# Seven block products instead of eight in all six feed-forwards, and a new order of the vector work

## The reference

```python
def swiglu(h, w1, w3, w2):
    return (jax.nn.silu(h @ w1) * (h @ w3)) @ w2
def half_ffn(x, g, w1, w3, w2):
    return x + FFN_RES * swiglu(rmsnorm(x, g), w1, w3, w2)     # four times in the first block
...
    for l in range(DEPTH):                                      # second block
        mod = (c_act @ w_ada[l] + b_ada[l])[:, None, :]
        sh1, sc1, g1, sh2, sc2, g2 = jnp.split(mod, N_MOD, axis=-1)
...
        x = x + g2 * swiglu_2(h, w_gate_up[l], w_down[l])
```

## Time and profile before

| | us |
|---|---|
| median of 3 runs (lowest, highest) | 3132.42 (3131.48, 3132.74) |
| the profiled execution | 3134.22 |
| its span, first to last instruction | 3132.4 |
| busy TensorE, VectorE, ScalarE | 3120.2, 2040.7, 1274.8 |

### The profile page before, as it was taken

One profiled execution on the slowest core, in us unless ns is written; L12 is line 12 of the kernel. 1 busy time (PEld: TensorE's weight loads), 2 busy tenths in 40 slices (PEclk: granted clock), 3 DMA queues, 4 the chain that ended last, 5 costly groups with the idle time before them and its releaser, 6 DMA issues.

```text
span 3132.4 us, 39304 instructions
## 1 busy us (share of the span) xinstructions
PE 3120.2 (100%) x15840; PEld 2629.8 (84%) x15840; DVE 2040.7 (65%) x3069; ACT 1274.8 (41%) x1908; POOL 156.5 (5%) x170
## 2 busy tenths in 40 slices
PE   9999999999999999999999999999999999999999
PEld 7888878888888888888888888887898988789898
DVE  5457567445755456647644575888893868889574
ACT  5322264322234222264332223556452545745342
POOL 2000000000000000000000000113000002400000
PEclk9999999999999999999999999999999999999999
DMA  5345422334542335422233454221223233022322
GB/s 151 94 134 180 136 85 88 101 94 135 189 141 82 104 125 168 155 94 82 81 100 102 135 181 146 69 81 39 83 95 118 86 103 97 15 94 94 109 92 84
DMA packets 334348, 340.00 MB, mean 109 GB/s; under 512 B 12503, under 2 KB 329209, under 8 KB 334169
## 3 DMA queue, kind: packets, MB, share of 16 engines
q1 hardware_dynamic: 332144, 333.80, 33.4%
q0 software_dynamic: 1792, 3.62, 0.4%
q10 hardware_dynamic: 232, 0.06, 0.0%
HBM read 335.36 MB, written 2.10 MB: 108 GB/s over the span
## 4 chain that ended last, share of the span: by engine, by line
PE 92%; DVE 4%; ACT 3%; DMA 0%; issue 0%; SPq 0%; DVEq 0%
PE ps L138 90%; PE ps L141 2%; ACT ar L95 1%; DVE wl L100 1%; DVE ar L108 1%; DVE ar L100 1%; ACT wh L95 0%; DVE hl L108 0%; DMA raw<-in_ffn_w 0%; DVE T L108 0%; ACT L95 0%; ACT sp L95 0%; ACT T L95 0%; DVE ar L123 0%; DVE ar L111 0%
## 5 line engine op out<-in xcount | busy, mean ns | idle before, releaser
L100 DVE TENSOR_TENSOR wl<-raw,wh 128x1024 fp32r<-128x1024 f32 (+3 forms) x709 | 728.4, 1030 | 421.0 <-ACT wh L95 418.9
L138 PE MATMUL ps<-hh,wl 128*128 128x512 f32 (+1 forms) x2632 | 991.7, 377 | 2.0 <-DVE wl L100 1.1
L138 PE MATMUL ps<-hh,wh 128*128 128x512 f32 (+1 forms) x2632 | 984.7, 374 | 0.0
L138 PE MATMUL ps<-hl,wh 128*128 128x512 f32 (+1 forms) x2632 | 984.3, 374 | 0.0
L95 ACT ACTIVATE wh<-raw 128x1024 fp32r<-128x1024 f32 (+3 forms) x709 | 628.4, 896 | 536.2 <-PE ps L138 458.7
L138 PE MATMUL ps<-ul,wh 128*128 128x512 f32 (+1 forms) x1664 | 585.4, 356 | 0.0
L138 PEld LDWEIGHTS ps<-hh,wl 128*128 128x128 f32 x2632 | 496.0, 188 | 95.9 <-issue 8.2
L138 PEld LDWEIGHTS ps<-hh,wh 128*128 128x128 f32 x2632 | 496.0, 188 | 88.9
L138 PEld LDWEIGHTS ps<-hl,wh 128*128 128x128 f32 x2632 | 496.3, 189 | 85.6 <-issue 0.2
L138 PE MATMUL ps<-uh,wl 128*128 128x512 f32 (+1 forms) x1568 | 557.3, 355 | 0.8 <-ACT sq L95 0.8
L138 PE MATMUL ps<-uh,wh 128*128 128x512 f32 (+1 forms) x1568 | 555.9, 354 | 0.0
(11 more groups left out here) (258 smaller groups left out, 2898.6 us busy)
## 6 DMA issues: line engine op xcount, KB each, us to landing
raw<-in_ffn_w SPq DMA_DIRECT2D x119, 1024.0 KB, 5.3
raw<-in_w_ada SPq DMA_DIRECT2D x48, 1024.0 KB, 5.2
raw<-in_w_gate_up SPq DMA_DIRECT2D x44, 1024.0 KB, 5.1
raw<-in_m_w_in SPq DMA_DIRECT2D x26, 1024.0 KB, 5.4
raw<-in_w_down SPq DMA_DIRECT2D x16, 1024.0 KB, 5.2
raw<-in_ffn_w SPq DMA_DIRECT2D x16, 768.0 KB, 4.9
raw<-in_w_in SPq DMA_DIRECT2D x12, 1024.0 KB, 5.4
raw<-in_m_w_out SPq DMA_DIRECT2D x8, 1024.0 KB, 5.2
```

What stands on the lines that cost most here:

```text
L100: return self.issue(lambda e: e.tensor_tensor(out, a, b, op))
L138: return self.issue(lambda e: e.matmul(out, l, r, start=start, stop=stop, skip_group_check=True))
```

## The change

WOVEN now holds the same 16 chunks for all six stages (32 before, 96 after), so the four ffn stages take the woven form with its two output parts. The description says 17 chunks; the set in the code has 16. ADA_AFTER becomes a table: 10 conditioning chunks in each ffn stage and 8 in ffn2 of layer 0, all in the first output part; the waits for them ask for number 23 in layer 0. The splits get due times of their own: blocks 6 and 5 one and two steps later, the mixes as entries of the same sorted list lo_order, and ScalarE goes by hi_order. The gates of ffn and ffn2 become a step of their own (`gated` on VectorE), done one step after the join, and the low parts two steps later (settle).

```diff
+WOVEN = {s: {("w3", 2), *((w, j) for j in range(3, 11) for w in ("w1", "w3"))} - {("w3", 10)} for s in FFNS}
 PARTS = (1, 4, 6, 5)
-ADA_AFTER = ({("post", "w3", 2 * j + 1) for j in range(7, 11)} | {("out", (k0, kt), 2 * m + 1) for m in range(3) for k0, kt in ((0, 8), (8, 8), (16, 6)) if m < 2 or k0 < 16},
-             {("post", "w3", 15), ("post", "w3", 19), *(("out", k, t) for k in ((0, 8), (8, 6)) for t in (1, 3, 5, 7)), ("out", (14, 8), 1), ("out", (14, 8), 3)})
+ADA_AFTER = {s: {("out", k, t): 1 + (s[0] == "ffn" and (k, t) in (((0, 8), 3), ((8, 6), 5))) for k in ((0, 8), (8, 6)) for t in (1, 3, 5, 7)}
+             for s in FFNS[:5]}
+ADA_AFTER[FFNS[5]] = {}
 SHARE = {1: (0, 0), 5: (0, 0), 3: (0, 0), 2: (1, 0), 4: (1, 1), 6: (1, 1), 7: (0, 1)}
 MOVING = {5: 0, 6: 1, 7: 2, 4: 3}
 BETWEEN = [("xb", 4), ("xb", 5), ("xb", 6), ("xb", 7), ("z", 2), ("z", 3)]
...
+        def plan_ffn(key, w1, w3, w2):
             at = {}
             for what, w, i, p in rounds(key):
                 j = i if what in ("part", "joined") else i // 2
...
             elif st[0] == "mix0":
                 W = I['m0_w_in'][0]
...
+        due = {g: before[g] + 1 for g in before}
+        for g, (s, w, j, p) in part_of.items():
+            if p in (6, 5):
+                due[g] = min(due[g] + (1 if p == 6 else 2), g - 2)
+        hi_order = sorted(due, key=lambda g: (due[g], g))
+        lo_order, last = [], 0
+        for o in order:
+            if o[0] == "ada":
+                lo_order.append((max(due[last], 2), last, 1, o))
+            else:
+                last = o[1]
+                lo_order.append((due[last], last, 0, o))
+        for g, (s, w, j, p) in part_of.items():
+            at_part = {c: due[G_of[(s, w, j, "part", c)]] for c in (1, 3, 4, 5)}
+            if p == 1:
+                lo_order.append((due[g], g, 1, ("mix", 7, part_of[g], shape[g][0])))
+            elif p == 4:
+                lo_order.append((due[g] + 1, -3, 0, ("mix", 6, part_of[g], shape[g][0])))
+                lo_order.append((due[g] + 1, -1, 0, ("mix", 5, part_of[g], shape[g][0])))
+            elif p == 3:
+                late = at_part[3] - 2 <= at_part[5]
+                lo_order.append((max(at_part[3] - 2, at_part[5]), g if late else -2, 1, ("mix", 3, part_of[g], shape[g][0])))
+        lo_order.sort(key=lambda c: c[:3])
...
-            mms = [o for o in order if o[0] == "mm"]
...
-                while at[0] < len(mms) and before[at[0]] < g:
-                    i = at[0]
+                while at[0] < len(hi_order) and due[hi_order[at[0]]] <= g:
+                    i = hi_order[at[0]]
...
-                for _ in range(3 if s == STAGES[0] else 4):
+                for _ in range(1 if s[0] == "ffn" else 4):
...
+                        dve.wait_ge(*left_of(("ada", 47 if s[1] else 23)))
                         if s[0] == "ffn2":
...
-
-                if p == 1:
-                    mix(7, 1, 7, SUB)
-                elif p == 4:
+            def mixed_weights(dst, chunk, n):
+
+                s, w, j, _ = chunk
+                a, b, op = {7: (1, 7, SUB), 6: (4, 7, SUB), 5: (6, 1, ADD), 3: (2, 6, SUB)}[dst]
+                if dst == 6:
                     dve.wait_ge(worked, (s, w, j, 7, "weights"))
                     dve.wait_ge(lo_split, G_of[(s, w, j, "part", 4)])
-                    mix(6, 4, 7, SUB)
-                    dve.own()
-                    mix(5, 6, 1, ADD)
-                elif p == 7:
+                elif dst == 5:
+                    dve.wait_ge(worked, (s, w, j, 6, "weights"))
+                    dve.wait_ge(lo_split, G_of[(s, w, j, "part", 1)])
+                elif dst == 3:
+                    dve.wait_ge(worked, (s, w, j, 6, "weights"))
                     dve.wait_ge(lo_split, G_of[(s, w, j, "part", 5)])
-                    mix(3, 2, 6, SUB)
+                dve.tt(quarter_of(n, dst), quarter_of(n, a), quarter_of(n, b), op).then_inc(worked, (s, w, j, dst, "weights"))
 
             def split_ahead(g):
 
...
-                    o = order[at[0]]
-                    if (before[o[1]] >= g) if o[0] == "mm" else (g < 2):
-                        return
+                while at[0] < len(lo_order) and lo_order[at[0]][0] <= g:
+                    o = lo_order[at[0]][3]
                     at[0] += 1
                     if o[0] == "mm":
                         hi, lo, src = split_views(o[1])
                         dve.wait_ge(hi_split, o[1])
                         dve.tt(lo, src, hi.bitcast(F32), SUB).then_inc(lo_split, o[1])
-                        if o[1] in part_of:
-                            mixed_weights(*part_of[o[1]], o[2])
+                    elif o[0] == "mix":
+                        mixed_weights(*o[1:])
                     else:
                         _, i, n = o
                         src = raw_view(n)
...
+
+            def gated(s, w, t):
+
+                to = (T1 if w == "w1" else T3)[t % 2][:, :]
+                done = (worked, (s, "odd", w, t // 2)) if t % 2 else left_of((s, "Y", w, t // 2))
+                dve.wait_ge(*done)
+                if w == "w1":
                     dve.tt(to, to, R[:, :], MUL).then_inc(worked, (s, "gate", t))
-                if w == "w3":
-                    dve.own()
+                else:
                     silu_done(s, t)
-                    dve.tt(to, to, T1[a][:, :], MUL).then_inc(worked, (s, "gv", t))
+                    dve.tt(to, to, T1[t % 2][:, :], MUL).then_inc(worked, (s, "gv", t))
 
             def differences(s):
-                if s != STAGES[0]:
+                if s[0] == "ffn2":
                     yield 1
                 for q in range(4):
...
+                    token = dve.beside(differences(s))
+                    if s[0] == "ffn":
+                        next(token)
+                        next(token)
                 chain, later = None, []
+
+                def settle():
+                    for c in list(later):
+                        c[0] -= 1
+                        if c[0] == 0:
+                            later.remove(c)
+                            if c[1] == "low":
+                                low_gated(s, c[2])
+                            else:
+                                gated(s, *c[1:])
+                                if c[1] == "w3":
+                                    later.append([2, "low", c[2]])
+
                 for what, w, i, p in rounds(s):
                     if what == "run":
                         product(s, w, i)
...
                     elif what == "joined":
                         joined(s, w, i, p)
-                        if w == "w3":
-                            later.append(2 * i + p)
+                        if w == "w3" or s[0] == "ffn":
+                            later.append([1, w, 2 * i + p])
                     elif what == "out":
...
-                        while later:
-                            low_gated(s, later.pop(0))
+                        settle()
+                        while later and p & 2:
+                            settle()
                         if p & 2:
                             added(s, nxt, i, p)
...
-                pool.wait_ge(used, G_of[(BEFORE[s], "w2", 14 if WOVEN[BEFORE[s]] else 0, 7)])
+                pool.wait_ge(used, G_of[(BEFORE[s], "w2", *((14, 0) if WOVEN[BEFORE[s]] else (0, 7)))])
```

More of the change, by code:

```diff
@@ L371, in plan_ffn @@
                     n_mm[0] += 1
-                if with_ada and (what, w, i) in ADA_AFTER[bool(WOVEN[key])]:
-                    plan_ada(1)
+                plan_ada(ADA_AFTER[key].get((what, w, i), 0))
         for st in STAGES:
             if st[0] == "ffn":
-                plan_ffn(st, I['ffn_w1'][st[1], st[2]], I['ffn_w3'][st[1], st[2]], I['ffn_w2'][st[1], st[2]], True)
+                plan_ffn(st, I['ffn_w1'][st[1], st[2]], I['ffn_w3'][st[1], st[2]], I['ffn_w2'][st[1], st[2]])
             elif st[0] == "mix0":
```

17 lines of the change are left out of this document (4 added, 13 removed).

## The result

| | before | after |
|---|---|---|
| median, us (lowest, highest) | 3132.38 (3131.48, 3132.74) | 3227.08 (3226.18, 3231.43) |
| the profiled execution, its span | 3134.22, 3132.4 | 3231.43, 3229.6 |
| busy TensorE, VectorE, ScalarE | 3120.2, 2040.7, 1274.8 | 3101.2, 2473.5, 1470.9 |

The change makes the kernel slower: ratio 1.0306, interval 1.0288 to 1.0323. The forecast was 3175, with a range of 3147 to 3200; it is 52 us short. The page of the changed kernel, for the earlier trace rows: span; busy time and count of the engines; the chain by engine; the group of the low splits, with VectorE's idle time before them and what ended it.

The account below looks back on a forecast made before the run. The prediction took VectorE's handing over with ScalarE to bound the woven rounds. From the profiled execution: 3134.2 - 52 + 71 + 11 + 2.5 + 8.6 + 2 = 3177.3; with the median 1.8 lower, 3175 us, range 3147 to 3200.

Parts of the forecast that it names:

- TensorE's part: 64 chunks go from plain to woven form, 10.90 to 10.08 us each: 52 us less if TensorE is fed.
- VectorE's round: Woven ffn chunks take 11.85 us, 1.77 over TensorE's 10.08, through waits for ScalarE: 71 us lost in four stages.
- A: TensorE stays the bound; waits for ScalarE fall into VectorE's free time in woven rounds: 3093 us, chance 0.07.
- B: One of the round's two waits is hidden because ScalarE takes its silu earlier: 3123 to 3147 us, chance 0.09.
- D: VectorE instructions cost their full duration in woven rounds, 0.687 for 0.604 us: 3244 us, chance 0.02.
- E: Matmuls of 256 columns cost 0.130 us, so seven products save nothing: 3145 us with rounds hidden, chance 0.01.
- the low part of tile 12: First output part: TensorE waits for it at the fifth tile of (8,6), 1.6 us in five stages, 8.6 in all.
- the part's account of 79.2 us: First output part: VectorE's conditioning, splits, additions and chunk ends sum to 78.5 of 79.2 us, so full.
- Rival C: First output part overflows, VectorE waiting for ScalarE and TensorE: 5 us more in each of four stages, 3195 us, chance 0.12.
- The first chunks and the constants: The first stage's constants, some 15 instructions at 0.16 us, stand in the woven rounds: 2.5 us.
- ffn2: Its woven chunks under the new order take 10.64 us, 0.56 over before's 10.08: 11 us lost in 20 steps.
- The gathering matmul: First output part: the reduce waiting for it makes a split 1 us late in ffn (0,1) and (1,1): 2 us.

Follow-up runs that it names:

- number 1: Changed kernel with ScalarE's silu (or high part of u) one step later, behind the next high splits, and VectorE's low part one step later: 3130.02 us.
- 4: Changed kernel with only the odd tile's silu (or high part of u) behind the next high splits on ScalarE, low part alike: 3173.99 us.
- number 2: Changed kernel with VectorE doing waiting gates and low parts ahead of splits and conditioning at the second output of each part: 3193.21 us.
- number 3: Changed kernel with both edits: ScalarE's silu behind the next high splits, and VectorE's gates and low parts ahead of the conditioning: 3097.55 us.
- Number 5: Changed kernel with the old WOVEN and old conditioning table, so the new order alone, the four ffn stages in plain chunks: 3150.66 us.

## Why the prediction was wrong, step by step

**TensorE's part** held: -52, and matmuls of 256 columns 0.120 us apart.

**VectorE's round** held in mechanism and size: 11.85 us forecast, 11.83 measured; waits of 1.31 and 0.70 forecast, 1.30 and 0.70 measured, both ended by ScalarE's wh; TensorE's gap before each block 6 was forecast at 1.8 and is 1.53 of idle time, 1.69 over the usual step. Numbers 1 and 4 show the chain by taking it away. Rivals A, B, D and E are out: A and B by the waits in each round, D by the starts 0.60 apart (1123.46, 1124.06), E by the 0.120.

**The term that failed is the low part of tile 12**: 1.6 us a stage forecast, 5.16 measured in the four ffn stages and 4.88 in ffn2 of layer 0, and behind it 1.5 to 2.9 from the clock (in ffn (1,0) 2.9: 13 matmuls 0.2 us slower, and the step between the levels). Only ffn2 of layer 1, which has no conditioning, came as forecast: 0.6, and 0.45 measured. The step was "that split can start only after that product [...] 1.4 + 1.2 for it, 1.0 for the transpose and reduce in the new order, 0.7 for itself". The chain was begun at the split of w2, as if the tile had its gate by then. But `gated` is a step of its own in the new order and `settle` comes after out_run, whose step holds 3.4 us of sums: block 2 was done by 1177.4, the join came at 1180.62 behind the conditioning and splits of the step before, and the gate 5.0 us behind the join. The second product of (0,8) ended at 1182.8; from there to TensorE's next start at 1190.87 are 8.1 us, where the step had 4.3. The prediction had counted these sums in the part's account of 79.2 us, where they fit, and not in this chain. Rival C put something of this size down to a full VectorE; it was not full, number 2 took the loss away with the same work in another order. The clock wasn't in the sum at all. What the lower level costs could have been read in the kernel before (0.43 us in place of 0.23 at 173.52); that a wait brings it on could not: past its first 20 us TensorE never waits there for more than 0.5 us. The first output parts came to 42.4 for 10.6.

**The first chunks and the constants** were priced by duration alone (15 x 0.16), as if the round were full from the third chunk on and free before it. The chain through ScalarE is there at the first woven chunks too (number 1 took some 8 us of it away), and in the first stage TensorE waits 3.12 and 2.74 us, with 2.8 and 1.7 behind them from the clock: +22 for 2.5. ScalarE's table loads stand in that stage as well, but not in the chain of the 3.12: behind the load ScalarE is idle until VectorE's tiles come. What makes the first stage worse than the others, and what the rest of this row is, stays open; number 3 still waits 3.11 us there. ScalarE in the changed kernel, ahead of the first of these waits and ahead of the second:

```profile
71.15 1.28 ACT L95 ACT_TABLE_LOAD   x1
73.26 0.63 ACT L95 ACTIVATE T<-T 128x512 f32<-128x512 f32 x1 [0.83 <-DVE T L100]
75.18 0.63 ACT L95 ACTIVATE T<-T 128x512 f32<-128x512 f32 x1 [1.29 <-DVE T L100]
...
91.77 1.28 ACT L95 ACT_TABLE_LOAD   x1
93.06 0.31 ACT L95 ACTIVATE small<-small 128x8 f32<-128x8 f32 x2
```

A load takes 1.28 us in the trace (the Trainium skill, ScalarE: Activation LUTs, "What ACT_TABLE_LOAD costs", says 1283 ns and about as much again for a drain; the next instruction, at 93.06, starts 0.01 us after the load here, so that no such second part shows).

**ffn2**: 10.64 us a chunk forecast, 10.83 measured; the waits were 0.62 and 0.54, then 0.28 and 1.22. With the first chunks it was 16.8 for 11. Number 5 confirms it, 18.8.

**The gathering matmul** was right: 1 late each in (0,1) and (1,1) forecast; 1.4 and 1.1 us over TensorE's own time found, of which 1.11 and 0.81 are the wait. VectorE and TensorE in ffn (0,1), the reduce waiting for the gathering matmul, then sums, then the split that TensorE waits for:

```profile
798.23 0.42 DVE L123 TENSOR_REDUCE adaq<-ada 128x8 f32<-128x256 f32 x1 [3.81 <-PE ps L138]
...
802.06 1.22 DVE L100 TENSOR_TENSOR wl<-raw,wh 128x1024 fp32r<-128x1024 f32 x1
```
```profile
803.42 0.47 PE L138 MATMUL ps<-uh,wl 128*128 128x512 f32 x1 [1.11 <-DVE wl L100]
```

One slip of arithmetic changes nothing: the differences of h are 12 x 1.2 = 14.4 us, not 14.6. Of the 56 us between the forecast sum of 43 and the 99 found, about 32 are the first output parts, 20 the first chunks and 6 ffn2.

## What to carry to other kernels

An order that parts an operation from the one it depends on also puts something in between: ask for each parted pair what the largest thing is that can stand there, on every stage of the program, not only in the steady round. In a ring of two engines the place in the second engine's queue decided here: what waits for the first engine must stand behind all that the first engine will want next. And a chain is to be followed from the product that opens it, instruction by instruction, not from the middle; the sum of busy time fitted here, 78.5 of 79.2 us, and said nothing of it.

## What the runs showed of the hardware

A wait of 1.5 us in every 11.8 left TensorE's granted clock at 1.00; one of 5.16 us was followed by some 6 us with most of them at the level of 1.2 GHz. The stretch differs from place to place: behind a wait of 5.15 us in ffn (0,1) the loss was 1.5 us, behind 5.16 in ffn (1,0) 2.9. In number 3 a wait of 3.11 us in the first stage was followed by such a stretch, too; TensorE's row there, and the window of TensorE alone behind it:

```profile
76.02 0.55 PE L138 MATMUL ps<-uh,wl 128*128 128x256 f32 x1 [3.11 <-DVE wl L100]
```
```profile
76.00:82.00 6.00, 5.98 (x28) 0.50 0.01 3
```

The products behind it took 2.7 us more than their time, so that the wait of 3.1 us cost 5.8 in all, and the one of 5.2 us in ffn (1,0) 8.1. In number 3, with this one long wait, the mean granted clock is 0.999, as before. A wait is not needed for it: sixteen matmuls of one column, without a pause, were followed by the lower level in the kernel before (173.00 to 176.40), and there eight matmuls of 512 columns took 1.6 us more than at the full clock.
